# Latent attention: two heads side by side, positional products in the row halves, scores issued behind the transposes

## The chip, the cores and the metric

The kernel runs on one core of a Trainium2 chip. The metric is the device time of one execution in microseconds (us), median of the runs. Engines are PE (TensorE, matrix products), DVE (VectorE), ACT (ScalarE), POOL (GpSimd) and SP (SyncE, which issues DMAs); PEld is TensorE's loading of weights.

## What is computed

The program is two blocks one after the other, each of two layers, on 512 tokens of width 1024. All but one part of it is unchanged. That part is the attention of the last layer (`causal_mla_attention`), in float32, with 8 heads:

```
for blk in range(s // 128):                       # 4 blocks of 128 queries
    lo, hi = blk * 128, (blk + 1) * 128
    sc = (q_nope[lo:hi] @ k_nope[:hi].T           # 128 features, own keys for each head
          + q_rope[lo:hi] @ k_rope[:hi].T) * scale  # 64 positional features, keys shared by heads
    sc = where(key <= query, sc, -inf)
    outs.append(softmax(sc) @ v[:hi])
return (concat(outs) * silu(gate)) @ w_out
```

## The kernel before

**Products.** Projections hold a weight as a high and a low part (`whi` made by ACT at L464, `wlo` by POOL at L432), and inputs likewise; each 128x128 tile costs three products of 512 columns (L844, L845, L846, function `product`). A strip is 8 such tiles, and `strip_part` issues two of them (six products). Products of the attention itself are plain float32; each call shows as two records in the trace.

**Units.** The attention has 32 units, one for a head and a block of 128 queries: `hh = un // 4`, `n = un % 4`. A unit has n+1 key blocks of 128. `qn`, `kn` hold 128 features a head; `qr[:, hh // 2, :]` holds the positional queries of two heads, one in rows 0 to 63 and one in rows 64 to 127; `krz[:, b, :]` holds the positional keys in the rows of half b and zeros in the other half, so that a product over 128 rows takes head b alone. `krz` is filled by two memsets and two adds at L1848 and L1849, within the latent projection.

**What each engine does for a unit, in its own order.** PE (L1275 to L1285): part un % 4 of gate strip un // 4 (`strip_part`, into bank NRM); `scores3(un + 3)` (L1257 and L1258, into bank un % 2, once VectorE has read unit un + 1); a wait for `p_ready` of unit un; its n+1 transposes (L1010, into bank 2 + un % 2); the products of unit un - 1 with the values (`values3`, L1267, n+1 calls, into bank SX or SY by head). DVE (L1896 to L1907): `masked_max3(un + 2)` (mask add L1878, maximum L1880, L1881); `normed3(un)` (reciprocal L1886, scaling L1887, which raises `p_ready`); at the second unit of a head `gated` of the head before (output times gate, L1892), at the third the low part of it (L1475); at the fourth the gate strip out of its bank (`scaled`, L1498). ACT (L816 to L828): `exp3(un + 2)` (L807), the copy of the transposed probabilities into `ev` (L821), and once a head the silu of a gate strip (L812, with a table load before it and one behind), the high part of the gated output (L485) and the high part of a weight strip. `gated` writes `sg` (SBUF), from which both parts are made. After the last unit follows the output projection `oout`, whose first strip waits for the low part of head k before its k-th tile.

**What sets the order.** Each engine works through its own list in order; semaphores tie them. `sc_ps`: scores done; `sc_out`: scores read by DVE; `p_ready`: probabilities scaled; `pt_ps`, `pt_ready`: transposed, copied; `o_ps`, `o_out`: output ready, gated; `x_hi`, `x_lo`: high and low parts.

Of the kernel before, what the change touches and what calls it, by code (L numbers as in the profile page):

```python
# [10 lines left out]
ALU = mybir.AluOpType  # L11
# [3 lines left out]
P = 128  # L15
TOK = 512
# [20 lines left out]
NB = TOK // P  # L37

RH, RDK = 8, 64
MH, MN, MR = 8, 128, 64  # L40
# [3 lines left out]
SLOTS = 4  # L44
# [79 lines left out]
def program(nc, a):  # L124

    with ExitStack() as top:
# [3 lines left out]
        def area(stack, name, shape, dt=F32):  # L130
            return stack.enter_context(nc.sbuf_tensor(name, shape, dt))


        ps = top.enter_context(nc.psum_tensor("ps", [P, 8, 512], F32))
        NRM, SX, SY, SZ = 4, 5, 6, 7
# [86 lines left out]
        with ExitStack() as st:  # L222
            qn = area(st, "qn", [P, MH, TOK])
            kn = area(st, "kn", [P, MH, TOK])
            qr = area(st, "qr", [P, 4, TOK])
            krz = area(st, "krz", [P, 2, TOK])
            kr = krz[:, 0, :]
            v3 = area(st, "v3", [P, NB, D])
            cm = area(st, "cm", [P, TOK])
            sm3 = area(st, "sm3", [P, SLOTS, TOK])  # L230
            with ExitStack() as st2:
                pair(st2, "L", 5)
            with ExitStack() as st2:
                sg3 = area(st2, "sg3", [P, KT, TOK])
# [109 lines left out]
        def pair_stats(pair, k):  # L344
            s0 = 2 * pair % SLOTS1
            return cols[:, 8 * s0:8 * (s0 + 2)].rearrange("p (s k) -> p s k", s=2)[:, :, 2 * k:2 * k + 2]

        MX, NG, SUM, RC = range(4)
        finpre, eps2 = cols[:, 0:KT], cols[:, KT:KT + 1]
        acc2 = cu[:, 2:]  # L350
# [99 lines left out]
        def _(act):  # L450
# [32 lines left out]
            def high(dst, m, src, scale=None):  # L483
                if scale is None:
                    nc.scalar.activation(X[dst][0][:, m, :], src, ACT.Copy).then_inc(x_hi, 1)  # L485
                else:
                    nc.scalar.activation(X[dst][0][:, m, :], src, ACT.Copy, scale=scale).then_inc(x_hi, 1)
                xs[0] += 1
# [313 lines left out]
                value(10 + m, v3, m, (SZ, NRM)[m % 2])  # L802

            def exp3(un):
                n, q0 = (un % NB + 1) * P, 8 * (un % SLOTS)
                asked()
                answer(nc.scalar.activation(sm3[:, un % SLOTS, 0:n], sm3[:, un % SLOTS, 0:n], ACT.Exp, bias=cols[:, q0 + 1:q0 + 2],  # L807
                                            scale=MSCALE, accum_out=cols[:, q0 + 2:q0 + 3]))
# [5 lines left out]
            exp3(0)  # L814
            exp3(1)
            for un in range(U3):  # L816
                n = (un % NB + 1) * P
                if un + 2 < U3:
                    exp3(un + 2)
                act.wait_ge(pt_ps, U1 + un + 1)  # L820
                nc.scalar.copy(ev[:, un % 2, 0:n], ps[:, 2 + un % 2, 0:n]).then_inc(pt_ready, 1)  # L821
                if un % NB == 0 and un:
                    gates(un // NB - 1)
                if un % NB == 1 and un > NB:
                    act.wait_ge(o_out, un // NB)
                    high("C", un // NB - 1, sg[:, :])
                if un % NB == 2:
                    ahead("mgate", un // NB)  # L828
            gates(MH - 1)
            act.wait_ge(o_out, MH)  # L830
            high("C", MH - 1, sg[:, :])
            post("oout")
            assert xs[0] == XT["oo"] + 8

# [2 lines left out]
        def _(pe):  # L837
# [170 lines left out]
            def transposes(src, bank, n=NB):  # L1008
                for k in range(n):
                    last = nc.tensor.transpose(ps[:, bank, k * P:(k + 1) * P], src[:, k * P:(k + 1) * P], C("ident"))  # L1010
                return last
# [236 lines left out]
                transposes(sm3[:, m % SLOTS, :], (SZ, NRM)[m % 2]).then_inc(vt_ps, 1)  # L1248
            pe.wait_ge(evac, OUT0["mgate"])

            def scores3(un):
                hh, n = un // NB, un % NB
                pe.wait_ge(rope_done, 19 + hh // 2 + 1)
                if un >= 2:
                    pe.wait_ge(sc_out, PAIRS + un - 1)
                keys, qs = (n + 1) * P, slice(n * P, (n + 1) * P)
                nc.tensor.matmul(ps[:, un % 2, 0:keys], qn[:, hh, qs], kn[:, hh, 0:keys], start=True, stop=False)  # L1257
                nc.tensor.matmul(ps[:, un % 2, 0:keys], qr[:, hh // 2, qs], krz[:, hh % 2, 0:keys], start=False, stop=True).then_inc(sc_ps, 1)  # L1258

            def values3(un):  # L1260

                hh, n = un // NB, un % NB
                pe.wait_ge(pt_ready, U1 + un + 1)
                if n == 0 and hh >= 2:
                    pe.wait_ge(o_out, hh - 1)
                for kb in range(n + 1):
                    last = nc.tensor.matmul(ps[:, SX + hh % 2, n * P:(n + 1) * P], v3[:, kb, hh * P:(hh + 1) * P], ev[:, un % 2, kb * P:(kb + 1) * P],  # L1267
                                            start=(kb == 0), stop=(kb == n))
                if n == NB - 1:
                    last.then_inc(o_ps, 1)  # L1270

            for un in range(3):
                scores3(un)
            pe.wait_ge(vt_done, 18)
            for un in range(U3):  # L1275
                strip_part("mgate", un // 4, un % 4, "A")
                if un + 3 < U3:
                    scores3(un + 3)
                pe.wait_ge(p_ready, U1 + un + 1)
                if un >= 2:  # L1280
                    pe.wait_ge(pt_ready, U1 + un - 1)
                transposes(sm3[:, un % SLOTS, :], 2 + un % 2, un % NB + 1).then_inc(pt_ps, 1)
                if un:
                    values3(un - 1)
            values3(U3 - 1)  # L1285
# [5 lines left out]
        def _(dve):  # L1291
# [545 lines left out]
            for m in range(5):  # L1837
                scaled("odd", 1 + m, kn[:, m, :])
                answered()
                add_square(m in (2, 4))  # L1840
                low("L", m, kn[:, m, :], gain("qa", m) if m < 3 else gain("kva", m - 3))
                if m == 1:
                    V.tensor_tensor(ev[:, 0, :], kr[:, :], rcos[:, :], ALU.mult)
                    dve.wait_ge(rope_ps, 19)
                    ch.link(V.tensor_tensor(ev[:, 1, :], ps[:, SX, :], rsin[:, :], ALU.mult))
                    for b in range(2):
                        r, z = slice(64 * b, 64 * b + 64), slice(64 - 64 * b, 128 - 64 * b)
                        V.memset(krz[z, b, :], 0.0)  # L1848
                        last = V.tensor_tensor(krz[r, b, :], ev[r, 0, :], ev[r, 1, :], ALU.add)  # L1849
                    last.then_inc(rope_done, 1)  # L1850
                if m == 2:
                    dve.wait_ge(nrm_ps, nrm[0] + 1)
                    start_sum()
# [19 lines left out]
            dve.wait_ge(in_cm, 16)  # L1873

            def masked_max3(un):
                n, q0 = (un % NB + 1) * P, 8 * (un % SLOTS)
                dve.wait_ge(sc_ps, PAIRS + un + 1)
                V.tensor_tensor(sm3[:, un % SLOTS, 0:n], ps[:, un % 2, 0:n], cm[:, TOK - n:TOK], ALU.add).then_inc(sc_out, 1)  # L1878
                dve.wait_ge(sc_out, PAIRS + un + 1)
                ch.link(V.tensor_reduce(cols[:, q0:q0 + 1], sm3[:, un % SLOTS, 0:n], AX_X, ALU.max))  # L1880
                ask(V.tensor_scalar(cols[:, q0 + 1:q0 + 2], cols[:, q0:q0 + 1], -MSCALE, None, ALU.mult))  # L1881

            def normed3(un):
                n, q0 = (un % NB + 1) * P, 8 * (un % SLOTS)
                answered()
                ch.link(V.reciprocal(cols[:, q0 + 3:q0 + 4], cols[:, q0 + 2:q0 + 3]))  # L1886
                V.tensor_scalar(sm3[:, un % SLOTS, 0:n], sm3[:, un % SLOTS, 0:n], cols[:, q0 + 3:q0 + 4], None, ALU.mult).then_inc(p_ready, 1)  # L1887

            def gated(hh):
                dve.wait_ge(o_ps, KT + hh + 1)  # L1890
                dve.wait_ge(silu_done, 8 + hh + 1)
                V.tensor_tensor(sg[:, :], ps[:, SX + hh % 2, :], sg3[:, hh, :], ALU.mult).then_inc(o_out, 1)  # L1892

            masked_max3(0)
            masked_max3(1)
            for un in range(U3):  # L1896
                if un + 2 < U3:
                    if un + 2 >= SLOTS:
                        dve.wait_ge(pt_ps, U1 + un + 3 - SLOTS)
                    masked_max3(un + 2)  # L1900
                normed3(un)
                if un % NB == 1 and un > NB:
                    gated(un // NB - 1)
                if un % NB == 2 and un > NB:
                    low("C", un // NB - 1, sg[:, :])
                if un % NB == NB - 1:
                    scaled("mgate", un // NB, sg3[:, un // NB, :], at=NRM)  # L1907
            gated(MH - 1)
            dve.wait_ge(o_out, MH)
            low("C", MH - 1, sg[:, :])  # L1910
            post("oout", ybuf3, "post1", 1)
            assert xs[0] == XT["oo"] + 8
        return nc
# [128 lines left out]
```

## Time and profile before

| | us |
|---|---|
| runs | 1970.55, 1968.54, 1969.08; median 1969.08 |
| profiled execution, its own time | 1969.26 |
| its span | 1967.3 |
| PE busy | 1865.1 (95%) |
| DVE, ACT, POOL busy | 897.5, 745.2, 868.2 |
| first score product to first product of `oout` | 1795.86 to 1902.49, 106.63; PE busy 106.22 of it |
| after that, output projection and final norm | 64.8 |

The attention stage lies between 1795.86 and 1902.49 us of the span. The records of products overlap, since one begins before the one ahead of it has ended; how long a product occupies PE is read from one start to the next.

### The profile page before, as it was taken

How to read it: one execution, taken by the hardware profiler on the slowest of the kernel's cores; microseconds unless marked ns; L12 is line 12 of the kernel's file. 1: busy time of each engine (PE TensorE's matmuls, PEld its weight loads, DVE VectorE, ACT ScalarE, POOL GpSimd, SP SyncE). 2: the span in 40 equal slices, each digit the busy share in tenths (PEclk: the TensorE clock that was granted, in tenths of full speed). 3: DMA queues.
4: the chain of work that ended last, by engine and by line, in shares of the span. 5: the costliest groups of instructions: out<-in, count | busy, mean ns of one | idle time of the engine just before them, and what ended most of it. 6: DMA issues, size and time to landing. Idle time of an engine off the chain costs nothing.

```text
span 1967.3 us, 24852 instructions
## 1 busy us (share of the span) xinstructions
PE 1865.1 (95%) x8760; PEld 1514.0 (77%) x8760; DVE 897.5 (46%) x1308; ACT 745.2 (38%) x1169; POOL 868.2 (44%) x1174
## 2 busy tenths in 40 slices
PE   5759999999999999999999999999999999799995
PEld 4757888888888767888888888777888878577784
DVE  7995232121225788532121126542355541556654
ACT  5523333232324467533232334423233332424651
POOL 1014555555555611555554545554444545262231
PEclk7569999999999999999999999999999999899998
DMA  4234333333333311233333332323232223131111
GB/s 154 49 96 130 106 96 96 98 95 96 101 92 96 112 57 33 86 96 97 97 96 96 96 96 92 101 76 87 85 86 86 75 86 96 48 107 54 43 43 43
DMA packets 49472, 171.04 MB, mean 87 GB/s; under 512 B 5968, under 2 KB 6352, under 8 KB 48752
## 3 DMA queue, kind: packets, MB, share of 16 engines
q1 hardware_dynamic: 47968, 167.06, 28.3%
q10 hardware_dynamic: 1424, 2.88, 0.5%
q8 instruction: 54, 0.88, 0.2%
q14 instruction: 26, 0.21, 0.0%
HBM read 161.27 MB, written 2.10 MB: 83 GB/s over the span
## 4 chain that ended last, share of the span: by engine, by line
issue 43%; POOL 38%; PE 11%; DVE 6%; ACT 1%; POOLq 1%; DMA 1%; SPq 0%; DVEq 0%; ACTq 0%
POOL wlo L432 38%; PE ps L844 2%; PE ps L846 2%; PE ps L845 2%; PE ps L1267 1%; PE ps L1258 1%; PE ps L1257 1%; DVE bt L319 1%; DVE E L320 1%; DVE E L318 1%; PE ps L1010 1%; DMA vsw<-vsb 0%; PE ps L892 0%; PE ps L884 0%; DVE zz L1391 0%
## 5 line engine op out<-in xcount | busy, mean ns | idle before, releaser
L432 POOL TENSOR_TENSOR wlo<-raw,whi 128x256 fp32r<-128x256 f32 x1152 | 856.7, 776 | 1035.4 <-ACT whi L464 1000.6
L464 ACT ACTIVATE whi<-raw 128x1024 fp32r<-128x1024 f32 x288 | 301.8, 1052 | 377.7 <-PE ps L846 375.4
L844 PE MATMUL ps<-Ch,whi 128*128 128x512 f32 x912 | 362.8, 398 | 0.5 <-POOL wlo L432 0.5
L846 PE MATMUL ps<-Ch,wlo 128*128 128x512 f32 x912 | 355.5, 390 | 0.0
L845 PE MATMUL ps<-Cl,whi 128*128 128x512 f32 x912 | 355.1, 389 | 0.0
L844 PE MATMUL ps<-Ah,whi 128*128 128x512 f32 x656 | 265.2, 404 | 9.7 <-DVE Al L1477 8.0
L846 PE MATMUL ps<-Ah,wlo 128*128 128x512 f32 x656 | 256.3, 391 | 0.0
L845 PE MATMUL ps<-Al,whi 128*128 128x512 f32 x656 | 256.0, 390 | 0.0
L844 PE MATMUL ps<-Bh,whi 128*128 128x512 f32 x640 | 250.2, 391 | 0.0
L846 PE MATMUL ps<-Bh,wlo 128*128 128x512 f32 x640 | 249.0, 389 | 0.0
L845 PE MATMUL ps<-Bl,whi 128*128 128x512 f32 x640 | 249.0, 389 | 0.0
L844 PEld LDWEIGHTS ps<-Ch,whi 128*128 128x128 f32 x912 | 171.2, 188 | 43.0 <-issue 5.9
L846 PEld LDWEIGHTS ps<-Ch,wlo 128*128 128x128 f32 x912 | 171.2, 188 | 36.4
L845 PEld LDWEIGHTS ps<-Cl,whi 128*128 128x128 f32 x912 | 171.4, 188 | 35.4 <-issue 1.4
L844 PEld LDWEIGHTS ps<-Ah,whi 128*128 128x128 f32 x656 | 123.7, 189 | 39.9 <-issue 13.4
L845 PEld LDWEIGHTS ps<-Al,whi 128*128 128x128 f32 x656 | 123.8, 189 | 26.8 <-issue 2.9
L846 PEld LDWEIGHTS ps<-Ah,wlo 128*128 128x128 f32 x656 | 123.5, 188 | 26.3
L845 PEld LDWEIGHTS ps<-Bl,whi 128*128 128x128 f32 x640 | 120.2, 188 | 25.6 <-issue 0.7
L844 PEld LDWEIGHTS ps<-Bh,whi 128*128 128x128 f32 x640 | 120.1, 188 | 25.6 <-issue 0.7
L846 PEld LDWEIGHTS ps<-Bh,wlo 128*128 128x128 f32 x640 | 120.1, 188 | 24.9
L1573 DVE TENSOR_TENSOR h<-ps,h 128x512 f32 x48 | 33.2, 692 | 216.4 <-PE ps L846 216.4
L617 ACT ACTIVATE sg<-ev 128x512 f32<-128x512 f32 x64 | 40.5, 632 | 212.2 <-DVE ev L1564 212.2
(337 smaller groups left out, 2091.4 us busy)
## 6 DMA issues: line engine op xcount, KB each, us to landing
raw<-in_w SPq DMA_DIRECT2D x288, 512.0 KB, 3.6
u<-in_xch SPq DMA_DIRECT2D x1, 2048.0 KB, 8.2
vsw<-vsb SPq DMA_DIRECT2D x16, 128.0 KB, 2.3
zsw<-zz SPq DMA_DIRECT2D x16, 128.0 KB, 2.3
h<-in_xfm SPq DMA_DIRECT2D x2, 1024.0 KB, 7.2
out<-h SPq DMA_DIRECT2D x8, 256.0 KB, 2.0
bB<-in_bc SPq DMA_DIRECT2D x1, 1024.0 KB, 10.2
bC<-in_bc SPq DMA_DIRECT2D x1, 1024.0 KB, 13.7
```

The lines of the kernel that those rows point to most:

```text
L318: eng.tensor_tensor(cols4(out), pws(pw), mat(x), ALU.mult)
L319: ch.link(eng.tensor_tensor(cols4(tr), pws(pi), mat(z), ALU.mult))
L320: return eng.tensor_tensor(out, out, tr, op)
L432: last = nc.gpsimd.tensor_tensor(wlo[:, r, cc], raw[:, r, cc], whi[:, r, cc].bitcast(F32), ALU.subtract)
L464: nc.scalar.activation(whi[:, slot, :], raw[:, slot, :], ACT.Copy).then_inc(hi_ready, 1)
L617: nc.scalar.activation(sg[:, :], ev[:, 0, :], ACT.Square)
L844: nc.tensor.matmul(out, whi[:, slot, w], xh, start=first, stop=False)
L845: nc.tensor.matmul(out, whi[:, slot, w], xl, start=False, stop=False)
L846: return nc.tensor.matmul(out, wlo[:, slot, w], xh, start=False, stop=last)
L1010: last = nc.tensor.transpose(ps[:, bank, k * P:(k + 1) * P], src[:, k * P:(k + 1) * P], C("ident"))
L1257: nc.tensor.matmul(ps[:, un % 2, 0:keys], qn[:, hh, qs], kn[:, hh, 0:keys], start=True, stop=False)
L1573: V.tensor_tensor(h[:, o, :], bank(name, j), h[:, o, :], ALU.add).then_inc(evac, 1)
```

## The change

Units are counted in pairs of heads: `unit3(un)` gives head 2 (un // 8) + un % 2 and block (un // 2) % 4, so units 2p and 2p+1 are the same block of two heads. The scores of a pair are issued together, first the two products over 128 rows, then the two positional ones, each over its own 64 rows (`qr[r]`, `kr[r]`), in two banks; one instruction signals for both. They wait until both units of the pair before are read. They stand behind the transposes of an odd unit, for the pair that begins three units further on. Positional keys are one plain tile, filled by one add; a pad keeps the addresses behind it. Outputs of heads turn through three banks (SX, SY, SZ), and gated outputs through `sg` and `std`. `gated` of the two heads of a pair comes at the first and second unit of the next pair of heads, their low parts at the second and third, with a wait for the low parts before.

```
--- before.py
+++ after.py
@@ -223,8 +223,9 @@
...
             qr = area(st, "qr", [P, 4, TOK])
-            krz = area(st, "krz", [P, 2, TOK])
-            kr = krz[:, 0, :]
+            krz = area(st, "kr", [P, TOK])
+            kr = krz[:, :]
+            area(st, "pad_k", [P, TOK])
             v3 = area(st, "v3", [P, NB, D])
...
@@ -345,6 +346,13 @@
...
 
+        def unit3(un):
+            return 2 * (un // (2 * NB)) + un % 2, un // 2 % NB
+
+        def gout(hh):
+            return (sg, std)[hh % 2][:, :]
+
+        OB = (SX, SY, SZ)
         MX, NG, SUM, RC = range(4)
...
@@ -802,7 +810,7 @@
...
             def exp3(un):
-                n, q0 = (un % NB + 1) * P, 8 * (un % SLOTS)
+                n, q0 = (unit3(un)[1] + 1) * P, 8 * (un % SLOTS)
                 asked()
...
@@ -814,21 +822,23 @@
...
             for un in range(U3):
-                n = (un % NB + 1) * P
+                n = (unit3(un)[1] + 1) * P
                 if un + 2 < U3:
...
                     gates(un // NB - 1)
-                if un % NB == 1 and un > NB:
-                    act.wait_ge(o_out, un // NB)
-                    high("C", un // NB - 1, sg[:, :])
+                if un % (2 * NB) < 2 and un >= 2 * NB:
+                    hh = unit3(un)[0] - 2
+                    act.wait_ge(o_out, hh + 1)
+                    high("C", hh, gout(hh))
                 if un % NB == 2:
...
             gates(MH - 1)
-            act.wait_ge(o_out, MH)
-            high("C", MH - 1, sg[:, :])
+            for hh in (MH - 2, MH - 1):
+                act.wait_ge(o_out, hh + 1)
+                high("C", hh, gout(hh))
             post("oout")
...
@@ -1248,38 +1258,42 @@
...
 
-            def scores3(un):
-                hh, n = un // NB, un % NB
-                pe.wait_ge(rope_done, 19 + hh // 2 + 1)
-                if un >= 2:
-                    pe.wait_ge(sc_out, PAIRS + un - 1)
+            def scores3(pair):
+                jp, n = pair // NB, pair % NB
+                pe.wait_ge(rope_done, 19 + jp + 1)
+                if pair:
+                    pe.wait_ge(sc_out, PAIRS + 2 * pair)
                 keys, qs = (n + 1) * P, slice(n * P, (n + 1) * P)
-                nc.tensor.matmul(ps[:, un % 2, 0:keys], qn[:, hh, qs], kn[:, hh, 0:keys], start=True, stop=False)
-                nc.tensor.matmul(ps[:, un % 2, 0:keys], qr[:, hh // 2, qs], krz[:, hh % 2, 0:keys], start=False, stop=True).then_inc(sc_ps, 1)
+                for b in range(2):
+                    nc.tensor.matmul(ps[:, b, 0:keys], qn[:, 2 * jp + b, qs], kn[:, 2 * jp + b, 0:keys], start=True, stop=False)
+                for b in range(2):
+                    r = slice(64 * b, 64 * b + 64)
+                    last = nc.tensor.matmul(ps[:, b, 0:keys], qr[r, jp, qs], kr[r, 0:keys], start=False, stop=True)
+                last.then_inc(sc_ps, 2)
 
...
 
-                hh, n = un // NB, un % NB
+                hh, n = unit3(un)
                 pe.wait_ge(pt_ready, U1 + un + 1)
-                if n == 0 and hh >= 2:
-                    pe.wait_ge(o_out, hh - 1)
+                if n == 0 and hh >= len(OB):
+                    pe.wait_ge(o_out, hh - len(OB) + 1)
                 for kb in range(n + 1):
-                    last = nc.tensor.matmul(ps[:, SX + hh % 2, n * P:(n + 1) * P], v3[:, kb, hh * P:(hh + 1) * P], ev[:, un % 2, kb * P:(kb + 1) * P],
+                    last = nc.tensor.matmul(ps[:, OB[hh % 3], n * P:(n + 1) * P], v3[:, kb, hh * P:(hh + 1) * P], ev[:, un % 2, kb * P:(kb + 1) * P],
                                             start=(kb == 0), stop=(kb == n))
...
 
-            for un in range(3):
-                scores3(un)
+            scores3(0)
+            scores3(1)
             pe.wait_ge(vt_done, 18)
...
                 strip_part("mgate", un // 4, un % 4, "A")
-                if un + 3 < U3:
-                    scores3(un + 3)
                 pe.wait_ge(p_ready, U1 + un + 1)
...
                     pe.wait_ge(pt_ready, U1 + un - 1)
-                transposes(sm3[:, un % SLOTS, :], 2 + un % 2, un % NB + 1).then_inc(pt_ps, 1)
+                transposes(sm3[:, un % SLOTS, :], 2 + un % 2, unit3(un)[1] + 1).then_inc(pt_ps, 1)
+                if un % 2 == 1 and un + 4 < U3:
+                    scores3(un // 2 + 2)
                 if un:
...
@@ -1843,11 +1857,7 @@
...
                     ch.link(V.tensor_tensor(ev[:, 1, :], ps[:, SX, :], rsin[:, :], ALU.mult))
-                    for b in range(2):
-                        r, z = slice(64 * b, 64 * b + 64), slice(64 - 64 * b, 128 - 64 * b)
-                        V.memset(krz[z, b, :], 0.0)
-                        last = V.tensor_tensor(krz[r, b, :], ev[r, 0, :], ev[r, 1, :], ALU.add)
-                    last.then_inc(rope_done, 1)
+                    V.tensor_tensor(kr[:, :], ev[:, 0, :], ev[:, 1, :], ALU.add).then_inc(rope_done, 1)
                 if m == 2:
...
@@ -1873,7 +1883,7 @@
...
             def masked_max3(un):
-                n, q0 = (un % NB + 1) * P, 8 * (un % SLOTS)
+                n, q0 = (unit3(un)[1] + 1) * P, 8 * (un % SLOTS)
                 dve.wait_ge(sc_ps, PAIRS + un + 1)
...
@@ -1881,7 +1891,7 @@
...
             def normed3(un):
-                n, q0 = (un % NB + 1) * P, 8 * (un % SLOTS)
+                n, q0 = (unit3(un)[1] + 1) * P, 8 * (un % SLOTS)
                 answered()
...
@@ -1889,7 +1899,8 @@
...
                 dve.wait_ge(silu_done, 8 + hh + 1)
-                V.tensor_tensor(sg[:, :], ps[:, SX + hh % 2, :], sg3[:, hh, :], ALU.mult).then_inc(o_out, 1)
+                dve.wait_ge(x_lo, xs[0])
+                V.tensor_tensor(gout(hh), ps[:, OB[hh % 3], :], sg3[:, hh, :], ALU.mult).then_inc(o_out, 1)
 
...
@@ -1899,15 +1910,17 @@
...
                 normed3(un)
-                if un % NB == 1 and un > NB:
-                    gated(un // NB - 1)
-                if un % NB == 2 and un > NB:
-                    low("C", un // NB - 1, sg[:, :])
+                if un >= 2 * NB:
+                    if un % (2 * NB) in (1, 2):
+                        low("C", un // (2 * NB) * 2 - 3 + un % (2 * NB), gout(un - 1))
+                    if un % (2 * NB) < 2:
+                        gated(un // (2 * NB) * 2 - 2 + un % (2 * NB))
                 if un % NB == NB - 1:
                     scaled("mgate", un // NB, sg3[:, un // NB, :], at=NRM)
-            gated(MH - 1)
-            dve.wait_ge(o_out, MH)
-            low("C", MH - 1, sg[:, :])
+            for hh in (MH - 2, MH - 1):
+                gated(hh)
+                dve.wait_ge(o_out, hh + 1)
+                low("C", hh, gout(hh))
             post("oout", ybuf3, "post1", 1)
...
```

## Rows read from the trace of the kernel before

**Rows 1.** A stretch: length, busy of PE, PEld, DVE, ACT, POOL; clock; DMA
```profile
1850.00:1865.00 15.00, 15.00 (x84) 12.04 (x82) 9.77 (x28) 9.80 (x20) 3.90 (x6) 1.00 0.13 36
```
**Rows 2.** Waits between 1790 and 1905: us in total, times, longest
```profile
PEld ps L1010 <- DVE sm L1887: 0.8, 3, 0.4
```
**Rows 3.** Timeline, PE, attention stage: start, length, instruction, [idle <-releaser]
```profile
1839.80 1.02 PE L1258 MATMUL ps<-krz,qr 128*128 128x512 f32 x2
...
1840.66 0.27 PE L1010 MATMUL ps<-cst,sm 128*128 128x128 f32 x1
...
1843.26 0.39 PE L1258 MATMUL ps<-krz,qr 128*128 128x128 f32 x2
...
1843.49 0.38 PE L1010 MATMUL ps<-cst,sm 128*128 128x128 f32 x2
...
1843.71 0.39 PE L1267 MATMUL ps<-ev,v 128*128 128x128 f32 x2
...
1845.33 0.59 PE L1257 MATMUL ps<-kn,qn 128*128 128x256 f32 x2
...
1848.98 0.81 PE L1258 MATMUL ps<-krz,qr 128*128 128x384 f32 x2
```
**Rows 4.** Timeline, PE, where 64-row products stand today
```profile
732.78 0.40 PE L846 MATMUL ps<-Ch,wlo 128*128 128x512 f32 x1
733.10 1.14 PE L1049 MATMUL ps<-k,q 64*128 64x256 f32 x8
734.17 0.50 PE L844 MATMUL ps<-Ch,whi 128*128 128x512 f32 x1
734.50 0.40 PE L845 MATMUL ps<-Cl,whi 128*128 128x512 f32 x1
...
1387.00 1.16 PE L1172 MATMUL ps<-q,k 64*128 64x128 f32 x16
...
1571.05 0.93 PE L1195 MATMUL ps<-q,acc 64*128 64x128 f32 x6
```
**Rows 5.** Timeline, DVE, attention stage
```profile
1840.93 0.69 DVE L1878 TENSOR_TENSOR sm<-ps,cm 128x512 f32<-128x512 f32 x1 [2.49 <-PE ps L1010]
...
1842.63 0.35 DVE L1887 TENSOR_SCALAR sm<-sm,cols 128x256 f32<-128x256 f32 x1
...
1843.88 0.28 DVE L1878 TENSOR_TENSOR sm<-ps,cm 128x128 f32<-128x128 f32 x1
...
1844.78 0.42 DVE L1887 TENSOR_SCALAR sm<-sm,cols 128x384 f32<-128x384 f32 x1
...
1846.12 0.69 DVE L1475 TENSOR_TENSOR Cl<-sg,Ch 128x512 fp32r<-128x512 f32 x1 [0.92 <-ACT Ch L485]
...
1846.73 0.42 DVE L1878 TENSOR_TENSOR sm<-ps,cm 128x256 f32<-128x256 f32 x1
...
1847.90 0.49 DVE L1887 TENSOR_SCALAR sm<-sm,cols 128x512 f32<-128x512 f32 x1
...
1849.90 0.56 DVE L1878 TENSOR_TENSOR sm<-ps,cm 128x384 f32<-128x384 f32 x1 [0.67 <-PE ps L1258]
...
1851.34 0.29 DVE L1887 TENSOR_SCALAR sm<-sm,cols 128x128 f32<-128x128 f32 x1
```
**Rows 6.** Timeline, DVE and PE, first wait of the stage
```profile
1803.46 0.35 DVE L1887 TENSOR_SCALAR sm<-sm,cols 128x256 f32<-128x256 f32 x1
...
1803.88 0.44 PE L1010 MATMUL ps<-cst,sm 128*128 128x128 f32 x2 [0.20 <-DVE sm L1887]
```
**Rows 7.** Timeline, ACT, the silu of a gate strip
```profile
1854.44 1.28 ACT L812 ACT_TABLE_LOAD   x1
...
1855.73 0.63 ACT L812 ACTIVATE sg<-sg 128x512 f32<-128x512 f32 x1
```
**Rows 8.** Timeline, DVE and PE, latent projection
```profile
1729.84 0.69 DVE L1487 TENSOR_TENSOR acc<-acc,sq 128x512 f32<-128x512 f32 x1 [1.31 <-ACT sq L793]
...
1733.05 1.02 PE L995 MATMUL ps<-acc,cst 128*128 128x512 f32 x2
```

## The prediction

> **What bounds the kernel now.** I read the times of stretches first. In the attention stage of the second block TensorE is busy for all of a stretch of 15 us, at full granted clock, while VectorE and ScalarE are each busy about two thirds of it [rows 1]. Then the waits of that stage: TensorE waited for VectorE's scaled probabilities three times, 0.8 us together, 0.4 at the longest [rows 2]. So here a microsecond of TensorE work is a microsecond of the kernel, as long as nobody makes it wait; and a wait given to it is paid in full. Last the timeline, for the length of each slot. Records overlap, so a slot is read from start to start: a float32 product of 512 columns is two records 0.43 apart, one of 128 columns two records 0.11 apart; 256 and 384 columns go by proportion, 0.22 and 0.32. A product with values takes two slots of 0.11, a part of a gate strip 1.40 (from 1843.71 plus two slots, to 1845.33) [rows 3].
>
> **Positional products in row halves.** Now each of 32 units has one over 128 rows, half of them zeros: two slots each, 16 x 4 sizes, 16 x (0.11+0.22+0.32+0.43) = 17.3 us. After, two heads go side by side on rows 0 to 63 and 64 to 127. The trace has this form: eight records of 64 x 256 in the two halves take 1.14 us, where one after the other they would take eight slots of 0.22; sixteen of 64 x 128 take 1.16, while six in one half alone take 0.93. So halves overlap and one half alone doesn't [rows 4]. I take two slots for a pair of heads instead of four: **-8.6 us**.
>
> **What going into halves and back costs.** From the start of the product before (732.78) to that of the second one behind (734.50) is 1.72 us. Without a change of form it would be 0.23 + 4 x 0.22 + 0.23, about 1.33. So one excursion costs 0.39 to 0.40: some 0.09 ahead, 0.10 in the first slot, 0.20 behind [rows 4]. The old kernel has none in this stage, the new one 16: 16 x 0.39 = **+6.2 us**. TensorE's own work: -2.4. The Trainium skill (TensorEngine Tiling, Key Properties) says that changing the tiling mode drains TensorE; by that rule, the trace agrees, with 0.39 us. Its page TensorE: Matmul & The Clock Gate (Measured speedup vs the span model) has some 4 ns per further tile and no price for a change of form; by that alone the sum would lose the 6.2 us.
>
> **The wait that the new order makes.** Now scores(un+3) stand ahead of the wait for the probabilities of unit un, so VectorE has a whole iteration in hand. After, the scores of a pair stand behind the transposes of an odd unit u. VectorE, in order, must add the mask to unit u+3 (which needs those scores), reduce it, and only then scale unit u+1, for which TensorE waits one strip part later. Count from the start of the last positional slot. TensorE: slot + 0.19 (way back) + values of u-1, 0.22 per key block, + strip part 1.40. VectorE begins at slot + 0.16 (a record outlasts its slot by that: 1.02 for two slots of 0.43) + 0.11 (end of record to the add, 1848.98+0.81 to 1849.90 [rows 3, 5]). TensorE thus arrives 1.32 + 0.22 x blocks behind VectorE's begin. From add to start of scaling took 0.90, 1.17, 1.44, 1.70 for 1, 2, 3, 4 key blocks, the scaling itself 0.29 to 0.49 [rows 5], and 0.06 more to TensorE (1803.46+0.35 to 1803.88; the first slot after a wait is 0.06 longer, 0.44 against 0.38 for two) [rows 3, 6].
> - u at block row 0: scores of 3 blocks. VectorE 1.44+0.35+0.06 = 1.85, TensorE 1.54: stall 0.31, with restart 0.37.
> - block row 1: 4 blocks. 1.70+0.42+0.06 = 2.18 against 1.76: 0.42, with restart 0.48.
> - block row 2: 1 block. 0.90+0.49+0.06 = 1.45 against 1.98: none.
> - block row 3: 2 blocks. 1.17+0.29+0.06 = 1.52 against 2.20: none.
> Four pairs of heads x 0.85 = **+3.4 us**. The odd unit behind then has 1.79 (or 2.12) of VectorE against 1.96 (or 2.29) of TensorE: covered by 0.1.
>
> **Gates and low parts.** gated for two heads now falls on units 0 and 1 of the next pair, low on units 1 and 2. Three of the four land behind transposes or the long scores, which hide them. The tightest: low of the even head waits for its high part on ScalarE, which stands behind copy, table load 1.28, silu 0.63 [rows 7] and takes 0.63 itself, 3.1 us after the transposes of unit 0; low and gated end by 4.6, and the scores of unit 4 come at 4.9. The low part of the odd head (0.69 us, L1475 in [rows 5]) falls in unit 2, between the scaled unit 2 and the mask of unit 5, just where cover is 0.1: 0.6 late, three times: **+1.7 us**. Its high part is long ready on ScalarE, and the third output bank removes a wait that does not show today. A wait for earlier low parts is added before gated; queued behind it is VectorE's next mask, 0.3 us early, so nothing. The last pair has both low parts in front of the output product; TensorE needs the last one only at its eighth k step, and by the same lengths it comes 0.3 us before: nothing.
>
> **The start.** Pair 1 of the scores waits until both units of pair 0 are read. Today four scores and a strip part run without a gap, and then comes the 0.4 us wait [rows 2, 6]. After: pair 0 until 0.96; the add of unit 0 begins at 1.1, that of unit 1 0.77 later, read at 2.2: TensorE idle 1.3. Pair 1 and the strip end at 5.3, and VectorE has scaled unit 0 at 5.5. Idle 1.4 against 0.4: **+1.0 us**. The end of the stage (copies behind a table load) I leave as it is.
>
> **Key rotation.** Two memsets and two adds become one add, 2 us less on VectorE. This is hidden both ways: the sum there is ready at 1730.5 while TensorE comes to use it at 1733.05 [rows 8]. No DMA and no strip load is moved, and the SP and POOL queues keep their order.
>
> **Sum.** -8.6 + 6.2 + 3.4 + 1.7 + 1.0 = +3.7. The profiled execution took 1969.26, so 1973.0; it stands 0.2 above the median of the runs, so I predict 1972.8. Bounds of the unknown terms: an excursion next to float32 products may cost 0.30 to 0.45 (-1.4 to +1.0); the stalls may be 0.1 shorter or 0.15 longer each (-1.1 to +1.7). Its own range: 1970.5 to 1975.2.
>
> **Rivals.**
> 1. **The waits are covered** (0.17). If VectorE starts 0.3 to 0.4 us earlier than I set, or ScalarE and VectorE overlap better, the eleven stalls vanish and only net work and start remain: -2.4 + 1.0, 1967.8. For it: today the wait is all but absent. Against: the order now puts a chain of 2.2 us into 1.8.
> 2. **Slower, VectorE's handover is the new bound** (0.18). Place: scaling of the even unit behind the mask of unit u+3, eight times, and the low part, three times. If each comes 0.2 us later than counted (gated, low and the odd unit have only 0.1 to 0.3 in hand, so delays add on), 11 x 0.2 = +2.2: 1975.0. It decides from 0.02 us per handover on, since the sum stands right at the bound.
> 3. **Change of form is free** (0.06), if the weights' load is hidden where the neighbours are float32 too: -6.2: 1966.6. With covered waits too (0.09): 1961.6. Against: the excursions shown pay, the one behind float32 values too [rows 4].
> 4. **Halves don't overlap with one product each** (0.03): +8.6, 1981.4. All examples shown have at least four products in a run.
> 5. **Forecast** (0.47).
>
> The clock could fall in the 1.3 us gap at the start; I give this no case of its own, it belongs to the top of the range.
>
> **Chances.** A measurement of this kernel can tell about 0.2%, 3.9 us, from no change: below 1965.1 is faster, above 1973.0 slower. The forecast case lies about half on each side: 0.24 same, 0.23 slower. Same: 0.24 + 0.17 + 0.06 = 0.47. Slower: 0.23 + 0.18 + 0.03 = 0.44. Faster: 0.09. The range 1967.6 to 1976.5 leaves out rival 3, alone and with covered waits, and rival 4: 0.18.
>
> **What would show it.** Positional records of 64 x n, starting in pairs, two slots for a pair of heads; about 0.39 us per excursion; TensorE waits for the scaling (now L1887) about eleven times, 0.3 to 0.6 us each, at the even unit behind scores of 3 and of 4 blocks and at unit 3 of a pair of heads; idle of 1.3 us behind the first pair. The stage from the first score to the first output product, 106.6 us today by the table ahead, should be 110.3. It would be wrong if the stage shows no waits for VectorE, or if stage length changes by another cause, such as ScalarE's copies coming late after its table loads.

## The result and the profile after

The changed kernel takes 1974.15 us (median of 10 runs, 1973.01 to 1975.98) against 1969.28 (10 runs, 1967.64 to 1970.94): ratio 1.0024, interval 1.0014 to 1.0034. It is slower by 4.9 us where 3.7 was forecast. The profiled execution took 1975.98, with a span of 1974.06.

Not all of the 6.7 us between the two spans is the change's. The first score product starts at 1797.09 instead of 1795.86; 1.1 of that 1.2 us arises within the first 170 us, in code that the change doesn't touch, and it comes and goes from run to run (the kernels below start the stage between 1793.7 and 1798.0). So I read the attention stage by itself, from the first score product to the first product of the output projection. This is the stretch view of the changed kernel, over the stage and over 15 us of it (columns as in [rows 1]):

```profile
1797.09:1908.95 111.86, 106.21 (x563) 75.33 (x561) 64.82 (x182) 69.03 (x135) 22.62 (x32) 1.00 0.11 34
1855.00:1870.00 15.00, 14.08 (x66) 8.82 (x64) 9.52 (x25) 8.99 (x18) 2.85 (x4) 1.00 0.19 51
```

The stage is 111.86 long instead of 106.63, **5.2 us more**, at the same full clock. Where TensorE was busy for all 15 us [rows 1] it now has 0.9 us without a product. The waits of the stage name who it waits for:

```profile
DVE sm L1888 <- PE ps L1271: 26.1, 16, 2.8
PEld ps L1020 <- DVE sm L1897: 9.2, 12, 1.2
PE ps L1268 <- DVE sm L1888: 1.3, 1, 1.3
```

Where the old kernel had three waits for the scaling, 0.8 us together [rows 2], this one has twelve, 9.2 together (weight loads wait earlier than products do, so this sum is longer than what is lost); and one of 1.3 at the start, for the scores of the first pair to be read. The first of these rows is the other half of the loop: VectorE waits for the positional products sixteen times, once a pair. The two wait for one another.

Next the timeline of TensorE for one pair of units with three key blocks, up to the wait behind it:

```profile
1831.06 1.46 PE L1268 MATMUL ps<-kn,qn 128*128 128x384 f32 x4
1832.44 0.92 PE L1271 MATMUL ps<-kr,qr 64*128 64x384 f32 x4
1833.29 0.49 PE L1281 MATMUL ps<-ev,v 128*128 128x128 f32 x2
1833.53 0.47 PE L854 MATMUL ps<-Ah,whi 128*128 128x512 f32 x1
...
1834.77 0.40 PE L856 MATMUL ps<-Ah,wlo 128*128 128x512 f32 x1
1835.32 0.44 PE L1020 MATMUL ps<-cst,sm 128*128 128x128 f32 x2 [0.16 <-DVE sm L1897]
```

Four positional records take 0.85 us from their start to the next product: two slots of 0.32 and 0.21 for the form. So two heads do go side by side. Ahead of them stand 1.38 for four slots of 0.32, 0.09 more than they need, and behind them the first product with values is 0.10 longer (0.49 for two, against 0.39 in [rows 3]). That is 0.40 for the excursion, with what rounding leaves. The last strip product starts at 1834.77 and lasts a slot of 0.23; the transposes start at 1835.32: 0.32 lost.

And VectorE for the same stretch, with POOL's row beside it:

```profile
1833.48 0.56 DVE L1888 TENSOR_TENSOR sm<-ps,cm 128x384 f32<-128x384 f32 x1 [0.32 <-PE ps L1271]
...
1834.91 0.35 DVE L1897 TENSOR_SCALAR sm<-sm,cols 128x256 f32<-128x256 f32 x1
1835.18 0.68 DVE L1489 TENSOR_TENSOR Cl<-std,Ch 128x512 fp32r<-128x512 f32 x1
1835.79 0.55 DVE L1888 TENSOR_TENSOR sm<-ps,cm 128x384 f32<-128x384 f32 x1
...
1837.21 2.86 POOL L440 TENSOR_TENSOR wlo<-raw,whi 128x256 fp32r<-128x256 f32 x4 [10.45 <-ACT whi L472]
1837.22 0.88 DVE L1897 TENSOR_SCALAR sm<-sm,cols 128x256 f32<-128x256 f32 x1
```

The mask waits for the scores, and the scaling that TensorE wants stands 1.43 behind it, as [rows 5] have it. Then comes the low part (L1489), which pushes mask and scaling of the next unit on by 0.6. One thing here was in no forecast: that scaling, of 256 columns, takes 0.88 instead of 0.35. It begins as POOL starts on a weight strip.

### The profile page after: what moved, and what is told of

It reads as the page before. It is cut to its first block, busy times and chain, and to the rows that moved or that the text cites. A ratio compares the mean times of both kernels' runs of the same rounds, so it can differ in the third digit from the quotient of the medians.

```text
span 1974.1 us, 24834 instructions
## 1 busy us (share of the span) xinstructions
PE 1867.5 (95%) x8760; PEld 1509.0 (76%) x8760; DVE 896.5 (45%) x1305; ACT 745.9 (38%) x1169; POOL 869.2 (44%) x1174
## 4 chain that ended last, share of the span: by engine, by line
issue 43%; POOL 38%; PE 10%; DVE 7%; ACT 1%; POOLq 1%; DMA 0%; SPq 0%; DVEq 0%; ACTq 0%
POOL wlo L440 38%; PE ps L854 2%; PE ps L856 2%; PE ps L855 2%; PE ps L1268 1%; PE ps L1281 1%; DVE bt L320 1%; DVE E L321 1%; PE ps L1020 1%; DVE E L319 1%; PE ps L1271 1%; DMA vsw<-vsb 0%; DVE cols L1890 0%; DVE sm L1888 0%; PE ps L902 0%
```

## Experiments

Stage lengths come from one profile of each kernel; medians are given against runs of the kernel before on the same chip: its median was 1969.81 beside runs 1 to 4 (21 executions, one of which took 5121.88 us, which a median does not feel) and 1970.57 beside runs 5 to 8 (30). The ratio given is not the quotient of the two medians, and the two differ by up to 0.07%.

**1. The row half alone, unpaired.** Kernel before, with

```
-  matmul(ps[:, un % 2, 0:keys], qr[:, hh // 2, qs], krz[:, hh % 2, 0:keys], ...)
+  r = slice(64 * (hh % 2), 64 * (hh % 2) + 64)
+  matmul(ps[:, un % 2, 0:keys], qr[r, hh // 2, qs], krz[r, hh % 2, 0:keys], ...)
```

> The kernel before, its order unchanged, with each unit's positional product over its own 64 rows instead of 128 rows half of zeros; nothing is paired, so nothing can overlap. Theory (each excursion into 64-row form and back costs TensorE 0.39 us): 32 excursions, +12.5 us, about 1981.8; the attention stage grows from 106.6 to 119.1, with few waits for VectorE. Rival (the form costs nothing, the change is slower by its waits alone): 1969.3, stage 106.6. If a one-half product were cheaper than a full one: below 1969.

1980.22, ratio 1.0057 (1.0044 to 1.0071); stage 117.38. No new wait for VectorE: the stage grew by 10.75 us with TensorE busy for 117.1 of it. The timeline of one unit:

```profile
1860.70 0.38 PE L1257 MATMUL ps<-kn,qn 128*128 128x128 f32 x2
1861.01 0.48 PE L1259 MATMUL ps<-krz,qr 64*128 64x128 f32 x2
1861.43 0.44 PE L1010 MATMUL ps<-cst,sm 128*128 128x128 f32 x2
1861.70 0.39 PE L1268 MATMUL ps<-ev,v 128*128 128x128 f32 x2
```

Without a change of form these four starts would be 0.22 apart; they are 0.31, 0.42 and 0.27 apart. So an excursion takes 0.34 here, and 32 of them 10.8: the whole difference. (The kernel before loses some 0.4 us at its first scaling [rows 2, 6] and this one doesn't, which would make it 0.35.) It is 0.05 cheaper than my 0.39, because a transpose follows instead of a product with values: its first slot is 0.05 longer and that of a product with values 0.10, as above. A product over 64 rows is no shorter than one over 128: from the start of the last of its records to the next product is the length of a full slot and 0.09 to 0.10 more, at 128 columns as at 512. The theory of a price per excursion stands; the rival that the form is free falls.

**2. The new order with full rows.** Changed kernel, positional products over 128 rows again (`krz`, two memsets and two adds as in the kernel before), everything else as changed.

> The changed kernel with its positional products back over 128 rows with zeros in the other half (two memsets and two adds as before), all else as changed: order, banks, gates. Theory: TensorE's own work +8.6 - 6.2 = +2.4; VectorE gets its scores 0.19 us later relative to TensorE's next wait, eight times, +1.5; 1978.1, stage 115.8 against 111.9. Rival (the row halves themselves are what made it slower): faster than 1974.2, down to 1970.

1980.22, ratio 1.0060 (1.0046 to 1.0073); stage 116.01. That is 4.15 more than with the halves, where the theory had 3.9: the halves are what the changed kernel gains by, and its order alone costs 9.4 us of stage over the kernel before.

```profile
PEld ps L1019 <- DVE sm L1899: 10.8, 12, 1.2
```

Twelve waits again, 1.6 us longer together: they come from the order, not from the form.

**3. The low part later.** Changed kernel, VectorE's list:

```
-                    if un % (2 * NB) in (1, 2):
-                        low("C", un // (2 * NB) * 2 - 3 + un % (2 * NB), gout(un - 1))
+                    if un % (2 * NB) in (1, 5):
+                        hh = un // (2 * NB) * 2 - 2 + un % (2 * NB) // 4
+                        low("C", hh, gout(hh))
```

> The changed kernel with the low part of the odd head moved from the third to the sixth unit of the next pair of heads, behind that unit's scaling. Theory (the low part stands in VectorE's queue ahead of the mask and the scaling that TensorE waits for, and pushes that scaling beside a POOL pass that slows it): the three waits of 0.94 us at the fourth unit go, -2.8 us, 1971.3, stage 109.0. If the slow scaling is from elsewhere: -1.7, 1972.5. Rival (TensorE waits there for ScalarE's table loads and copies, not for VectorE's queue): no change, 1974.2.

1971.78, ratio 1.0011 (1.0002 to 1.0021); stage 108.84, 3.0 less. The three waits are gone, and with them the slow scalings: none takes over 0.5 us. The other eight waits stay as they were, 0.31 to 0.43.

**4. Scaling an even unit first.** Changed kernel:

```
+                if un % 2 == 0:
+                    normed3(un)
                 if un + 2 < U3:
                     ...
                     masked_max3(un + 2)
-                normed3(un)
+                if un % 2:
+                    normed3(un)
```

> The changed kernel; VectorE scales an even unit ahead of the mask of the unit two further on instead of behind it; odd units as they were. Theory (an even unit's scaling doesn't need the new scores, it only stands behind their mask): the eight waits of 0.32 and 0.43 us and their restarts go, -3.4 us; the three by the low part stay or shrink by up to 0.4 each; 1970.3, stage 108.0. Rival (the chain scores, mask, exp, copy is the bound whatever its order): the waits move to the odd units and the time stays at 1974.2, or grows as ScalarE's copies stand behind later exponentials.

1970.54, ratio 1.0006 (0.9997 to 1.0015); stage 106.53, 5.3 less, more than I had written down. All eight waits went, and the three by the low part shrank from 0.94 to 0.36 to 0.38, since the scaling that meets POOL's start is now that of the even unit behind (0.80 instead of 0.42), which TensorE wants a strip part later.

```profile
PEld ps L1020 <- DVE sm L1897: 1.9, 3, 0.6
PE ps L1268 <- DVE sm L1888: 1.3, 1, 1.3
```

This is the run that carries the explanation: the same instructions on every engine, two steps exchanged in VectorE's list, and the stage is back at the length it had before the change. That it is the same to 0.1 us is chance: TensorE's own work gives 2.4, the start takes 1.1 and the three waits that are left, with restarts, 1.3. The chain of scores, mask and exponential was never too long; one scaling that needs nothing of it stood behind it.

**5. Both moves together.**

> Both moves of VectorE's order in one kernel: an even unit scaled ahead of the next mask, and the low part of the odd head at the sixth unit. Theory: of the waits for VectorE only the one at the start is left; the three of 0.36 us with their restarts in the kernel that scales first go: stage 105.3 against 106.5 there, 106.6 before; 1969.3. Rival (the waits only move on to ScalarE's copies or to later masks): stage stays at 106.5.

1969.51, ratio 0.9993 (0.9984 to 1.0002); stage 105.31, as expected to 0.1; the median is 0.2 above what was written down.

**6. And the start.** On top of 5: the scores of the second pair go to banks SX and SY, and its mask adds read them there.

```
-                if pair:
+                if pair == 1:
+                    pe.wait_ge(rope_done, 23)
+                elif pair:
                     pe.wait_ge(sc_out, PAIRS + 2 * pair)
+                b0 = SX if pair == 1 else 0
```

> The same, and the scores of the second pair written to two of the output banks, which stand empty at the start, so that they needn't wait until the first pair is read. Theory: the 1.3 us wait at the start goes and the wait for the first scaling grows by some 0.3: stage 104.2, which is 2.4 us under the kernel before, so the net of the row halves (-8.6 + 6.2) stands alone at last; 1967.6 to 1968.3. Rival (VectorE takes the first four units no sooner, and the wait moves behind the first strip part): stage 105.3.

1967.21, ratio 0.9986 (0.9977 to 0.9995); stage 103.96. TensorE, by the stretch view again, stands still nowhere in the middle:

```profile
1794.80:1898.76 103.96, 103.57 (x563) 76.28 (x561) 64.87 (x182) 67.34 (x135) 22.96 (x32) 1.00 0.12 36
1850.00:1865.00 15.00, 15.00 (x74) 10.19 (x74) 10.13 (x28) 10.11 (x20) 2.93 (x4) 1.00 0.19 60
```

What is left, 0.39 us without a product, lies at the end of the stage, in a wait for ScalarE's copy. The start gave 1.35, more than the 1.1 expected: the wait for the first scaling, which is absent in run 5, was feared to come back and didn't. The median is 0.4 below what was written down. This kernel is faster than both, by 0.14% of the kernel before.

**7. The same with full rows.** As 6, with `krz` as in 2.

> The same again with positional products over 128 rows with zeros in the other half. Theory (halves give 8.6 and take 6.2 where nothing waits): 2.4 us more than with halves, stage 106.6. Rival (an excursion costs more than it gives once no wait covers it): equal or less than 104.2.

1970.15, ratio 0.9996 (0.9987 to 1.0005); stage 106.56. The stretch view of the stage:

```profile
1797.35:1903.91 106.56, 106.01 (x562) 82.46 (x561) 65.78 (x182) 67.30 (x135) 22.99 (x32) 1.00 0.12 35
```

With no wait in the middle, the row halves are worth 106.56 - 103.96 = 2.6 us of stage, against -8.6 + 6.2 = -2.4 counted. Of these 2.6, 0.16 are not TensorE's work but a longer wait for ScalarE's copy at the end (0.55 us without a product here, 0.39 in run 6); the busy times differ by 106.01 - 103.57 = 2.44, which is the sum counted.

**8. POOL's strip later.** Changed kernel, `ahead("mgate", un // NB)` at `un % NB == 3` instead of 2.

> The changed kernel with ScalarE's high part of a weight strip, and so POOL's low part, one unit later (at the fourth unit of four instead of the third). In the changed kernel the scaling of the fourth unit takes 0.88 us instead of 0.35 each time it begins together with POOL's first pass. Theory (POOL's pass slows a scaling that begins beside it): those three scalings are back at 0.35 and the waits there fall from 0.94 to 0.57, stage 110.8 against 111.9. Rival (VectorE's own low part just ahead slows it): they stay at 0.88 and the stage at 111.9.

1975.20, ratio 1.0024 (1.0014 to 1.0035): no gain in time; stage 110.30, 1.6 less. The timeline of VectorE and of POOL at the same place:

```profile
1834.47 0.68 DVE L1489 TENSOR_TENSOR Cl<-std,Ch 128x512 fp32r<-128x512 f32 x1
1835.07 0.55 DVE L1888 TENSOR_TENSOR sm<-ps,cm 128x384 f32<-128x384 f32 x1
...
1836.50 0.35 DVE L1897 TENSOR_SCALAR sm<-sm,cols 128x256 f32<-128x256 f32 x1
...
1838.79 2.83 POOL L440 TENSOR_TENSOR wlo<-raw,whi 128x256 fp32r<-128x256 f32 x4 [10.27 <-ACT whi L472]
```

With POOL 2.3 us away the scaling takes 0.35, though VectorE's own low part stands before it as it did. So it is POOL's pass that slows it, not the low part. TensorE's wait at this place, from the changed kernel (first two rows) and from this one:

```profile
1836.97 0.39 PE L856 MATMUL ps<-Ah,wlo 128*128 128x512 f32 x1
1838.15 0.44 PE L1020 MATMUL ps<-cst,sm 128*128 128x128 f32 x2 [0.79 <-DVE sm L1897]
...
1836.26 0.40 PE L856 MATMUL ps<-Ah,wlo 128*128 128x512 f32 x1
1836.91 0.44 PE L1020 MATMUL ps<-cst,sm 128*128 128x128 f32 x2 [0.25 <-DVE sm L1897]
```

Less a slot of 0.23, the three waits fell from 0.94 to 0.42, further than the 0.57 written down. What that gave was partly lost behind the stage, where the last strip's high part now stands before the last gate on ScalarE and the last low part comes late:

```profile
1912.45 0.50 PE L854 MATMUL ps<-Ch,whi 128*128 128x512 f32 x1 [0.75 <-DVE Cl L1489]
```

That one wait is about 0.9 us (1911.31 to 1912.45 less a slot of 0.23). The remaining 0.7 us is less than medians of this kernel tell apart.

## Why the prediction was right

| step | counted | measured in the changed kernel |
|---|---|---|
| halves side by side | -8.6 | two slots for a pair of heads, as counted |
| excursions | 16 x 0.39 | 0.40 at the pair shown, 0.39 at others; net of both steps -2.4 of TensorE's work, -2.6 of stage (runs 6, 7), against -2.4 |
| wait behind scores of 3 blocks | 0.31 | 0.31 to 0.33 |
| wait behind scores of 4 blocks | 0.42 | 0.42 to 0.43 |
| restart | 0.06 | 0.05 to 0.06 |
| block rows 2 and 3 | none | none |
| low part of the odd head | 3 x 0.57 | 3 x 0.99 with restart |
| start | +1.0 | +1.1 |
| stage | +3.7 | +5.2 |

**The mechanism was right step by step**, the even units' waits to 0.02 us, and run 4 shows that they are VectorE's order and nothing else. The likeliest case came in, 1.0 us above its number by the ratio (0.0024 x 1969.3 = 4.7 against 3.7), 1.2 by the medians.

**The term that was mis-sized is the low part of the odd head**: I counted 0.57 us each, it took 0.99. The step read "0.6 late, three times", with the scaling behind it at the 0.35 of [rows 5]. That row was taken where POOL was not starting. The pushed scaling lands in POOL's first pass, ends only behind it and takes 0.53 longer, and all of that reaches TensorE: in run 8, with the low part where it was and the scaling at 0.35, the wait is 0.52 shorter. There the low part costs 0.42 a time, with restart 0.48, which is 0.09 less than counted: the forecast's own 1.96 against 1.79 leaves 0.17 in hand, and it wrote 0.1. So two errors stand against each other, 3 x 0.52 = 1.6 that the sum did not have and 3 x 0.09 = 0.3 that it had too much; together they are 1.3 of the 1.5 us that the stage is over the forecast. Runs 3 and 8 take the slow scaling away in two ways. The sentence "no strip load is moved" was true of the list and beside the point: it was VectorE's instruction that moved onto a load that stayed.

**The waits are covered** (rival 1) didn't happen; run 4 shows what it would have taken. **The handover as bound** (rival 2) had the right place and a wrong cause: the eight handovers were on time to 0.02 us, and what came on top came at the three low parts alone. **Change of form is free** (rival 3) fell in run 1, **no overlap with one product each** (rival 4) in the trace. The Trainium skill (TensorEngine Tiling, Key Properties) says that a change of tiling mode drains TensorE. The trace agrees in that going and coming back costs 0.34 to 0.40 us; it splits this into 0.09 each way, a first slot in the halves longer by 0.10, and a first slot behind them longer by 0.05 to 0.10.

**Key rotation** is one add instead of four instructions, and lies ahead of the stage. Runs 6 and 7 differ in it too: their medians are 2.9 apart and their stages 2.6, so it gives or costs no more than medians can tell.

## What to carry to other kernels

When work on the bound engine is shortened by reordering it, write down for every other engine what then stands in its list between the new arrival and the next thing that is waited for; what needs nothing of the arrival goes in front. Two exchanged steps of VectorE's list were worth 5.3 us of stage here, twice what the row halves gain. A change of form on TensorE cost 0.34 to 0.40 us here whatever the columns (0.39 below), so it pays by the columns between going and coming: by these slots pairs of 4 key blocks gain 0.86 - 0.39, and those of one block lose, 0.22 - 0.39 (worked out; no run here mixes the forms).

## What the runs showed that was not expected

A scaling on VectorE that begins inside a pass of POOL ends only behind the end of that pass. This is one pass of the changed kernel's strip, alone:

```profile
1837.21 0.73 POOL L440 TENSOR_TENSOR wlo<-raw,whi 128x256 fp32r<-128x256 f32 x1 [10.45 <-ACT whi L472]
```

The pass ends at 1837.94, and the scaling of 256 columns that began at 1837.22 ends at 1838.10, 0.88 long; so in all three places (0.86 to 0.88 instead of 0.35). In run 4 POOL is held up too. VectorE's scalings there, with POOL's first and second pass, each in a row of its own:

```profile
1836.59 0.35 DVE L1897 TENSOR_SCALAR sm<-sm,cols 128x256 f32<-128x256 f32 x1
1836.68 0.86 POOL L440 TENSOR_TENSOR wlo<-raw,whi 128x256 fp32r<-128x256 f32 x1 [10.15 <-ACT whi L472]
1837.51 0.73 POOL L440 TENSOR_TENSOR wlo<-raw,whi 128x256 fp32r<-128x256 f32 x1
1837.65 0.80 DVE L1897 TENSOR_SCALAR sm<-sm,cols 128x384 f32<-128x384 f32 x1
```

The first scaling began 0.09 ahead of POOL and takes its usual 0.35; the pass takes 0.86 instead of 0.73. The second began inside a pass that ends at 1838.24; it ends at 1838.45 and takes 0.80 instead of 0.42. Here whoever comes second waits. A pass that begins late in a scaling does not, though: in the kernel before six passes begin 0.33 us into a scaling of 0.49 (at 1848.23 for the one of 1847.90 [rows 5]) and take 0.74 to 0.75, as other passes do. Nor is every instruction of VectorE held up: in the kernel before, POOL runs from 1848.23 to 1851.06, and inside it the mask add at 1849.90 [rows 5] and the maximum at 1850.49 take 0.56 each, as elsewhere. No scaling of the kernel before begins inside a pass of POOL, so none of its rows in the stage had this.

The kernel before does have it ahead of the stage, in additions with both inputs in SBUF. This is the last addition of the rotation of positional queries, first inside POOL's passes, then with POOL standing still:

```profile
1785.67 1.26 DVE L1504 TENSOR_TENSOR qr<-ev 128x512 f32<-128x512 f32 x1
...
1795.30 0.69 DVE L1504 TENSOR_TENSOR qr<-ev 128x512 f32<-128x512 f32 x1
```

The statement at L1504 takes 1.22 to 1.27 us in the three places where it begins inside a pass and 0.69 in the nineteen where none runs. So the warning stood in the trace that the forecast was made from.

The Trainium skill has a rule for it (page SBUF — State Buffer, sections Terms and SBUF: two separate sides): VectorE's second pair of ports is GpSimd's too and is locked for a whole instruction, so that whoever is second stands still; VectorE asks for it only in its modes with two ports, or with two inputs from SBUF. The trace agrees for the scaling, which waits and makes POOL wait, for the additions with two inputs from SBUF, which wait, and for the mask add (one input from PSUM) and the maximum, which don't. It does not bear out "for a whole instruction" in the six passes above, which begin inside a scaling and are not longer. No run here tried the scaling in another mode, so the lock as cause is argued, not shown; that POOL's pass is what slows it is shown (run 8).
